# Stick-breaking attention: the weighted values of a pair's two heads issued together, on both column halves of the array

## The reference, cut to what matters

```python
logits = jnp.einsum("bhtd,bhsd->bhts", q, kb) * (Dh ** -0.5)
mask = s_idx[None, :] < t_idx[:, None]
log_keep = jnp.where(mask, jax.nn.log_sigmoid(-logits), 0.0)
after = jnp.sum(log_keep, axis=-1, keepdims=True) - jnp.cumsum(log_keep, axis=-1)
wts = jnp.where(mask, jnp.exp(jax.nn.log_sigmoid(logits) + after), 0.0)
outs.append(jnp.einsum("bhts,bhsd->bhtd", wts, vb))
...
o = o * jax.nn.silu(z)
return o.astype(h.dtype) @ w_out
```

## Time and profile before

| | |
|---|---|
| time, median of 3 runs | 1438.62 us (1436.43 to 1439.15) |
| span of the profiled execution (its page gives no other time) | 1436.6 us |
| PE busy | 1348.6 us (94% of the span) |
| PE weight loads busy | 1037.2 us (72%) |
| ACT busy | 565.2 us (39%) |
| DVE busy | 472.6 us (33%) |
| POOL busy | 398.5 us (28%) |
| mean granted clock of PE | 0.973 of full |
| attention stage, from the first L1903 to the first L1541 that reads `yB_hi` | 769.5 to 918.3 us |

### The profile page before, as it was taken

One profiled execution on the slowest core, in us unless ns is written; L12 is line 12 of the kernel. 1 busy time (PEld: TensorE's weight loads), 2 busy tenths in 40 slices (PEclk: granted clock), 3 DMA queues, 4 the chain that ended last, 5 costly groups with the idle time before them and its releaser, 6 DMA issues.

```text
span 1436.6 us, 17837 instructions
## 1 busy us (share of the span) xinstructions
PE 1348.6 (94%) x7266; PEld 1037.2 (72%) x7266; DVE 472.6 (33%) x844; ACT 565.2 (39%) x926; POOL 398.5 (28%) x162
## 2 busy tenths in 40 slices
PE   6699999999999988999998999898999999999979
PEld 3588867789888866777775555676887777777747
DVE  0755532342342321334221333213112233242541
ACT  3343458432233522344344566323313434553410
POOL 0343431311124443233332000033223313335131
PEclk9899999999999989999999999999999999999969
DMA  9333311234442012222312000022213321224001
GB/s 334 110 88 104 100 59 59 89 118 147 137 129 89 2 59 88 71 85 83 109 64 88 0 0 1 1 88 94 88 53 109 93 70 60 88 71 179 16 0 59
DMA packets 102978, 117.82 MB, mean 82 GB/s; under 512 B 4560, under 2 KB 88944, under 8 KB 102904
## 3 DMA queue, kind: packets, MB, share of 16 engines
q1 hardware_dynamic: 98640, 112.21, 24.0%
q10 hardware_dynamic: 4264, 4.57, 1.1%
HBM read 111.52 MB, written 2.10 MB: 79 GB/s over the span
## 4 chain that ended last, share of the span: by engine, by line
PE 86%; ACT 6%; DVE 5%; issue 2%; ACTq 0%; DMA 0%; DVEq 0%
PE ps L1541 46%; PE ps L1635 4%; PE ps L2054 3%; PE ps L1769 3%; PE ps L1917 3%; PE ps L1784 3%; PE ps L1930 2%; PE ps L1903 2%; PE ps L1782 2%; PE ps L1624 2%; PE ps L1920 2%; PE ps L2023 1%; PE ps L1851 1%; PE ps L1846 1%; PE ps L2010 1%
## 5 line engine op out<-in xcount | busy, mean ns | idle before, releaser
L427 POOL TENSOR_TENSOR wlo<-raw,whi 128x2048 fp32r<-128x2048 f32 x58 | 267.2, 4607 | 697.5 <-ACT whi L550 685.1
L550 ACT ACTIVATE whi<-raw 128x2048 fp32r<-128x2048 f32 x56 | 106.9, 1911 | 264.6 <-PE ps L1541 229.6
L1635 PE MATMUL ps<-work,cs 128*128 128x512 f32 x160 | 78.4, 610 | 4.3 <-ACT work L555 4.1
L578 ACT ACTIVATE rbuf<-ps,cs 128x512 f32<-128x512 f32 x59 | 40.0, 679 | 63.4 <-PE ps L1635 48.7
L435 POOL TENSOR_TENSOR wlo<-raw,whi 128x2048 fp32r<-128x2048 f32 x10 | 46.3, 4634 | 66.8 <-ACT whi L614 66.8
L1314 DVE SCALAR_TENSOR_TENSOR nlk<-ps,att 128x1280 f32<-128x1280 f32 x16 | 23.9, 1492 | 118.9 <-ACT att L851 118.9
L444 POOL COPY yib<-cs 128x512 f32<-128x512 f32 x40 | 24.1, 615 | 122.6 <-PE ps L1784 122.6
L1784 PE MATMUL ps<-XT,yib 128*128 128x128 f32 x320 | 57.7, 276 | 0.0
L1541 PE MATMUL ps<-hC_hi,whi 128*128 128x512 f32 x208 | 55.1, 407 | 0.0
L939 ACT ACTIVATE p<-sc,nmx 128x256 f32<-128x256 f32 x64 | 32.1, 502 | 57.8 <-DVE nmx L1382 57.8
L1917 PE MATMUL ps<-nlk,cs 128*128 128x512 f32 (+3 forms) x128 | 48.1, 458 | 6.0 <-DVE after L1324 6.0
(11 more groups left out here) (367 smaller groups left out, 2972.1 us busy)
## 6 DMA issues: line engine op xcount, KB each, us to landing
raw<-in_w_in_dram SPq DMA_DIRECT2D x24, 1024.0 KB, 5.2
raw<-in_w_in_a_dram SPq DMA_DIRECT2D x16, 1024.0 KB, 5.6
raw<-in_w_ada_dram SPq DMA_DIRECT2D x16, 1024.0 KB, 5.2
raw<-in_w_ada_kv_dram SPq DMA_DIRECT2D x8, 1024.0 KB, 5.5
raw<-in_w_kv_dram SPq DMA_DIRECT2D x8, 1024.0 KB, 5.2
raw<-in_w_in_b_dram SPq DMA_DIRECT2D x8, 1024.0 KB, 5.4
ada_a<-in_w_ada_dram SPq DMA_DIRECT2D x4, 1024.0 KB, 8.3
ada_b<-in_w_ada_dram SPq DMA_DIRECT2D x4, 1024.0 KB, 10.7
```

The costliest lines, as they stand in the source:

```text
L427: pool.tensor_tensor(wlo[:, s, :], raw[:, s, :], whi[:, s, :].bitcast(F32), ALU.subtract).then_inc(lo_ready, 1)
L550: A(whi[:, s, :], raw[:, s, :], ACT.Copy).then_inc(hi_ready, 1)
L578: A(rbuf[:, g % 2, :], ssbank(g), ACT.Ln, scale=1.0 / width, bias=epsc).then_inc(ss_read, 1)
L1635: mm(ssbank(g), stat, work4[:, n % 4, :], start=first, stop=last).then_inc(sq_used, 1)
```

## The change

The weighted values are no longer done after each head but once for a pair, at the odd steps: at step n = 3, 5, ..., 17 `weighted((n-3)//2)` issues, for each key block, the product of the even head and then that of the odd head. The two write different halves of the partitions of one bank, and so use different halves of the array's output columns, with different `att` slots as moving data. The even steps are left with `suffix_sums(n-1)` and `qk(n+1)` alone. `pv_full` now counts pairs.

`att` gets four slots so that both heads of a pair stay. It moves to a new place that lies over the second slots of `whi` and `wlo` and over `work4`, `tmpu` and `rbuf`; `nlk` of odd heads and `after0` lie over the second slot of `whi`. So the second unit of `D_OUTB` cannot be split ahead of the stage any more: its `split_hi` on ACT moves from ahead of the table load to after the head loop, ahead of the last `yb_hi`, and its `split_lo` on POOL waits in addition for `pv_full` of pair 6.

```diff
+        with ExitStack() as scope:
+            sb("pad_w0", [128, 2048], F32, scope)
+            nlk1 = sb("nlk1", [128, 1280], F32, scope)
+            after0 = sb("after0", [128, 384], F32, scope)
+            sb("pad_w1", [128, 3200], F32, scope)
+            att = sb("att", [128, 4, 1280], F32, scope)
+            after1 = sb("after1", [128, 256], F32, scope)
...
                 for s in range(2):
+                    if (d, s) == (D_OUTB, 1):
+                        pool.wait_ge(pv_full, KD - 1)
                     split_lo(d, s)
...
-            copies(D_ZB + 1, lambda j: zsT[:, 4 + j, :], gate_done, ACT.Silu)
+            next_hi(D_ZB + 1, 0)
+            for j in range(4):
+                act.wait_ge(dense_full, 4 * (D_ZB + 1) + j + 1)
+                A(zsT[:, 4 + j, :], dense[j], ACT.Silu).then_inc(gate_done, 1)
...
             def head_exps(n):
-                a = att[:, n % 3, :]
+                a = att[:, n % 4, :]
                 act.wait_ge(qk_full, n + 1)
-                if n >= 3:
-                    act.wait_ge(pv_full, n - 2)
+                if n >= 4:
+                    act.wait_ge(pv_full, (n - 4) // 2 + 1)
...
+            next_hi(D_ZB + 1, 1)
             yb_hi(KD - 1)
             out_squares(D_OUTB, SQ_C, 8)
...
             def yb(kt):
-                dve.wait_ge(pv_full, 2 * kt + 2)
+                dve.wait_ge(pv_full, kt + 1)
...
-            def weighted(n):
-                s, kt, rs = n % 2, n // 2, slice(64 * (n % 2), 64 * (n % 2) + 64)
-                pe.wait_ge(wt_done, 2 * n + 2)
-                if kt >= 2 and n % 2 == 0:
+            def weighted(kt):
+                pe.wait_ge(wt_done, 4 * kt + 4)
+                if kt >= 2:
                     pe.wait_ge(yb_done, kt - 1)
                 for j in range(NT):
-                    last = mm(ps[rs, 6 + kt % 2, 128 * j:512], Vb[:, j, 64 * n:64 * n + 64],
-                              att[:, n % 3, off[j]:off[j] + 512 - 128 * j], start=j == 0, stop=True, skip_group_check=True)
+                    for n in (2 * kt, 2 * kt + 1):
+                        rs = slice(64 * (n % 2), 64 * (n % 2) + 64)
+                        last = mm(ps[rs, 6 + kt % 2, 128 * j:512], Vb[:, j, 64 * n:64 * n + 64],
+                                  att[:, n % 4, off[j]:off[j] + 512 - 128 * j], start=j == 0, stop=True,
+                                  skip_group_check=True)
                 last.then_inc(pv_full, 1)
...
-                if n >= 2:
-                    weighted(n - 2)
+                if n >= 3 and n % 2:
+                    weighted((n - 3) // 2)
                 if n + 1 < HB:
                     qk(n + 1)
```

More of the change, by code:

```diff
@@ L137, in mixer_stack @@
             with ExitStack() as s2:
-                att = sb("att", [128, 3, 1280], F32, s2)
-                after1 = sb("after1", [128, 256], F32, s2)
-            with ExitStack() as s2:
                 sc2 = sb("sc2", [128, 2, 512], F32, s2)
@@ L194, in mixer_stack @@
             zsT = sb("zsT", [128, KD, T], F32, B)
-            nlk = sb("nlk", [128, 2, 1280], F32, B)
+            nlk0 = sb("nlk0", [128, 1280], F32, B)
             ybt = sb("ybt", [128, 2, 512], F32, B)
-            after0 = sb("after0", [128, 384], F32, B)
-            pad_b = sb("pad_b", [128, KD * T - 3968], F32, B)
+            sb("pad_b", [128, KD * T - 2304], F32, B)
             with ExitStack() as s2:
@@ L238, in mixer_stack @@
             vst = sb("vst", [128, 2, 512], F32, Cc)
+        nlk = (nlk0, nlk1)
         ps = ctx.enter_context(nc.psum_tensor("ps", [128, 8, 512], F32))
@@ L854, in head_weights @@
                 act.wait_ge(sfx_full, n + 1)
-                A(att[:, n % 3, cols], logits(n % 2)[:, cols], ACT.Exp).then_inc(wt_done, 1)
+                A(att[:, n % 4, cols], logits(n % 2)[:, cols], ACT.Exp).then_inc(wt_done, 1)
             def logits(s):
@@ L1313, in _ @@
                     dve.wait_ge(sfx_full, n - 1)
-                STT(nlk[:, s, :], logits(s), 0.0, att[:, n % 3, :], ALU.max, ALU.add).then_inc(nlk_done, 1)
-                k1, k3, k2 = nlk[:, s, 512:896], nlk[:, s, 896:1024], nlk[:, s, 1024:1280]
+                STT(nlk[s][:, :], logits(s), 0.0, att[:, n % 4, :], ALU.max, ALU.add).then_inc(nlk_done, 1)
+                k1, k3, k2 = nlk[s][:, 512:896], nlk[s][:, 896:1024], nlk[s][:, 1024:1280]
                 dve.wait_ge(nlk_done, n + 1)
@@ L1913, in suffix_sums @@
                 pe.wait_ge(after_done, n + 1)
-                later = {0: after0[:, :], 1: after1[:, :], 2: nlk[:, s, off[3]:off[3] + 128]}
+                later = {0: after0[:, :], 1: after1[:, :], 2: nlk[s][:, off[3]:off[3] + 128]}
                 for j in range(NT):
                     width = 512 - 128 * j
-                    last = mm(logit_cols(s, off[j], width), C("negtri"), nlk[:, s, off[j]:off[j] + width],
+                    last = mm(logit_cols(s, off[j], width), C("negtri"), nlk[s][:, off[j]:off[j] + width],
                               start=False, stop=True, skip_group_check=True)
```

## The result

| | before | after |
|---|---|---|
| time, median | 1437.53 us (4 runs, 1436.18 to 1439.15) | 1456.39 us (4 runs, 1456.09 to 1456.69) |
| ratio, 95% interval | | 1.0128 (1.0114 to 1.0142) |
| time and span of the profiled execution | -, 1436.6 us | 1456.48, 1454.7 us |
| mean granted clock of PE | 0.973 | 0.959 |
| attention stage, first qk to first product of `D_OUTB` | 148.8 us | 166.7 us |

The kernel became 18.9 us slower. In the two profiled executions the span grew by 18.1 us, the attention stage by 17.9.

The account below looks back on a forecast made before the run. It took the attention stage to be bound by PE, with the ACT and DVE loop just behind. Terms -4.1 - 0.3 + 12.4 + 3.7 = +11.7 on 1436.6 gave 1448.3, median 1450.3, range 1437 to 1457 us.

Parts of the forecast that it names:

- The pair on both halves: Weighted values at odd steps: a pair side by side takes 2.30 us, so an odd step stays at 8.49 us.
- The even steps: Seven steps lose 2.30 us of PE work, but the ACT/DVE loop limits the gain to 0.58 each, 4.1 us.
- The clock: PE idles twice in each even step; one clock fall of 1.77 us in each of seven, +12.4 us.
- Step 16 and step 1: Stage's ends: step 16 has no qk, waits for the 4.27 us loop and gains nothing; step 1 got no term.
- The earlier start: Start of the attention stage: without the ACT split ahead of it, Abs(0) starts earlier, -0.3 us.
- The tail: Stage's end: POOL's moved split runs beside `yb_low` and delays the dense products, +3.7 us; bounds 0 and 4.6.
- The moved loads and splits: Second `D_OUTB` unit: later ACT and POOL splits and SP reloads still come in time for PE, no cost.
- the clock holds: Rival for the even steps: gaps under 1 us don't lower the clock, the 12.4 us vanish, 1437.9; chance 0.11.
- the halves don't overlap: Rival for the pair's products: an odd step takes 10.79 us, 16.1 more than the forecast, 1466; chance 0.02.
- POOL doesn't stop `yb_low`: Rival for the stage's end: the clock falls but the tail is free, 1446.6; chance 0.08.
- The rule of the Trainium skill: PE's clock in even steps: only long idle gaps lower it, so it would hold and 12.4 us be missing.

Follow-up runs that it names:

- the parted pair: Changed kernel with key block 0 of both heads' weighted values issued between an even step's qk products: 1435.94 us; with POOL's split after the last `yb_low`, 1430.12 us.

## Why the prediction was right, and what it mis-sized

- *The pair on both halves*: right. 2.31 us for sixteen passes, odd steps 8.50.
- *The even steps*: right in kind. With no fall one takes 8.03 us, as the kernels with filled gaps show, not 7.91, so the gain is 0.46 us each and not 0.58; 3.2 us instead of 4.1. One reading was short, with nothing hanging on it: in the 4.40 us of the earlier trace rows PE does 3.01 us of work and not 2.68, as the mask's 0.33 belong to it.
- *The clock*: right in mechanism, and shown by the filled gaps. This is the term that was too small. I took one fall of 1.77 us in each of seven even steps, 12.4 us. All seven fell, but four of them for 6.8 us. The seven steps take 73.9 us against 7 x 8.03 = 56.2: the term is 17.7 us. A single fall costs 1.57, a double one 3.24. I had said that misses and doubles should roughly cancel, but nothing missed. The double stretch was in the rows, as the upper bound, and four doubles are just where the stated range ends: 1456.39 is 0.6 us inside it, and a fifth double would have left it. That it was not one more is luck; no row could tell how many would double.
- *Step 16 and step 1*: step 16 falls in after (9.72 for 8.03), which I had left out; step 1, which fell before, does not (8.03 for 9.72). They cancel. Why step 16 falls in after, where PE's wait is as long as before (2.00 us, 2.01 before), stays open.
- *The earlier start*: -0.3 us came (9.15 us from the first qk to suffix sums(0), 9.41 before) and was lost to the clock in those sums: the first weights start 14.57 us after the first qk, 14.61 before.
- *The tail*: right. Forecast +3.7, measured 3.57 at PE and 3.55 by undoing it.
- *The moved loads and splits*: right, no cost. With the split later still, behind the last `yb_low`, PE found its unit ready.

The terms as measured: -3.2 + 17.7 + 3.5 give 18.0; the stage grew by 17.9. The forecast of the span was +11.7 and it grew by 18.1: the clock's term makes 5.3 of the 6.4 missing, the even steps 0.9. The rival that the clock holds is refuted, as are that the halves don't overlap and that POOL doesn't stop `yb_low`. The rule of the Trainium skill (TensorE: Matmul & The Clock Gate, "Why this matters for your kernels") on long idle gaps, by which 12.4 us would have been missing, doesn't cover this kernel. Here the clock fell in seven of seven even steps with gaps of 0.69 and 0.74 us and a 64-row product between them, and held once they were filled.

## What to carry to other kernels

Freeing the busiest engine gains only up to the next loop behind it, so measure that loop in the trace before counting the work removed: here 2.30 us removed in a step were worth 0.46. The matrix engine's clock can turn such a saving into a loss, because the freed time is idle time; put work into the gap that has to be done anyway, here the part of a product whose operands are ready first. And when a move puts a long POOL instruction beside DVE, look whether DVE's instructions there read both operands from SBUF.

## What the runs showed of the hardware

- Full clock does not need a PE without gaps. With the parted pair it was busy for 109.6 of 117 us at 1.00, with an open gap of 0.7 us in every even step.
- Short gaps can lower it: over 792 to 918 us PE was busy for 116.0 of 126 us and the mean was 0.85. Useless products in those gaps brought back 18.7 us. The same two gaps do not always lower it: with the pair's products head by head three even steps of seven kept full clock. Whether it matters that qk is only 64 rows deep was not tested.
- A DVE subtraction with both operands in SBUF that starts beside a running POOL split ends after it: 5.03 and 4.94 us for two that take 1.47. In the parted pair, with 5.58 us for the two, the first started 0.08 us ahead of POOL and took its 0.68; the second, begun beside POOL, ended 0.55 us after it. A DVE product that reads the accumulators is not slowed (0.69 us).
- Passes of 64 output columns on alternate halves, with different moving data, run at the pace of one: 2.31 us for sixteen, 3.93 us when the first head's eight are all issued ahead of the second's.
